# Eight of sixteen stretches of attention probabilities turned in blocks, the blocks carried by ScalarE and GpSimd

## The chip, the cores and the metric

The kernel runs on one NeuronCore of a Trainium2 chip. The core has a matrix engine (TensorE, PE in the profile), three engines for elementwise work (VectorE or DVE, ScalarE or ACT, GpSimd or POOL) and a queue engine that starts transfers (SyncE or SP). The metric is the device time of one execution in microseconds (us), as the median of three runs.

## The reference, cut to what matters

Two sequences of 512 tokens (here "trunks") go through one encoder layer with the same weights: a neighbourhood attention with 16 heads of 64 on a grid of 8 rows by 64 columns, then a mixture of 16 experts in which each expert picks its 64 best tokens of each trunk.

```
def trunk(x, ...):
    u = rmsnorm(h, norm_mix_g[i])
    mix = neighbourhood_attention(u, na_w_qkv[ia], na_rpb[ia], na_w_o[ia])
    h = h + mix
    u = rmsnorm(h, norm_ffn_g[i])
    h = h + expert_choice_ffn(u, router_w[i], moe_w_gate[i], moe_w_up[i], moe_w_down[i])
    return rmsnorm(h, final_norm_g)

def neighbourhood_attention(h, w_qkv, rpb, w_o):
    qkv = jnp.einsum('btd,de->bte', h, w_qkv)
    ...
        s = jnp.einsum('bchd,bicjhd->bhcij', q_r, k_win).astype(jnp.float32) + bias[None]
        p = jax.nn.softmax(s.reshape(B, NA_HEADS, GRID_W, kh * NA_KW), axis=-1)
        ...
        return jnp.einsum('bhcij,bicjhd->bchd', p, v_win)
    ...
    return jnp.einsum('btd,de->bte', out, w_o)
```

## The kernel before

**The parts.** The first 450 us or so are the attention of trunk 0 and then of trunk 1. The rest is the experts: sixteen passes over the weights, a loop of the same instructions. The change touches the attention alone.

**Precision.** Every float32 operand of a large product is split in two parts of a shorter format, a high part and a rest. ScalarE makes the high part (a cast, L870 for weights), VectorE the rest (a subtraction, L1404 for weights, `rest_pair`), and TensorE sums three products of parts. The weights come in slots of 128 x 2048 (a "pair": `q`, `k`, `v` or `w` with the number of its group); a slot is loaded again when its rest is made.

**Groups.** The 16 heads of a trunk go in four groups of four (`first_group` to `last_group`, one function on each engine). In each group TensorE projects the next group's queries and keys, and in turns the values (`project_v`) and the output (`project_out`). Within a group there are two pairs of heads (p = 0 and 1), and a pair is worked in two halves (hh = 0, 1 and hh = 2, 3). So there are 2 trunks x 4 groups x 2 pairs = 16 stretches.

**One stretch.** TensorE makes scores (`score`, L2193). VectorE adds the bias and takes the maximum (`biased`, L1478, L1482). ScalarE takes exponentials (`exponentials`, L895). VectorE multiplies with one over the sum (`normalise_rows`, L1498, L1501). Now the probabilities have queries on partitions, and the product with the values needs keys there: they have to be turned. There are two ways.
- In whole: TensorE transposes 28 pieces into PSUM (`turn_probabilities`, L2199), and VectorE and ScalarE copy one half each back to SBUF (`copy_pt`, L1486 and L900). 12 stretches go this way.
- In blocks: VectorE transposes blocks of 32 x 32 within their own 32 partitions (`turn_blocks_pt`, L1492), and ScalarE then carries 16 pieces of 32 partitions to the partitions where they belong (`move_pt`, L909). 4 stretches go this way, the first pair of the first and of the third group (`by_blocks`).

Then TensorE multiplies with the values (`values`, L2258), and the result is split (`split_ot`: high part by ScalarE, L934, rest by VectorE, L1518) for the output projection.

**Order.** Each engine runs its list in the order in which it is written, and waits on semaphores: `pt_dve`, `pt_act` and `pt_moved` say that turned probabilities are there, `norm_done` that normalised ones are. In the third group of trunk 0, ScalarE and VectorE also work out the root mean square of trunk 1's input (`next_piece`, `root`, `mean_square`, `one_over_rms`), for which ScalarE loads another table of functions (ACT_TABLE_LOAD). GpSimd does little in the attention: it clears a few tiles, starts transfers of its own queue, and waits.

Of the kernel before, what the change touches and what calls it, by code (L numbers as in the profile page):

```python
# [32 lines left out]
HEADS = 16  # L33
# [85 lines left out]
def by_blocks(n):  # L119

    return n % HEADS // GROUP % 2 == 0 and n % GROUP < PAIRED
# [59 lines left out]
ROW_BANKS = (4, 6)  # L181


def encoder_kernel(nc, x, x_t, g_mix, g_ffn_col, g_ffn, g_fin, w_qkv, bias, w_o, router_w, w_gate, w_up, w_down, identity, y):
# [5 lines left out]
    with ExitStack() as ctx:  # L190
# [3 lines left out]
        def sem(name):  # L194
            return ctx.enter_context(nc.semaphore(name))
# [231 lines left out]
        third_early, third_used = sem("third_early"), sem("third_used")  # L427
# [73 lines left out]
        def head_count(b, g):  # L501
            return HEADS * b + GROUP * g

# [210 lines left out]
        def _(pool):  # L714
# [11 lines left out]

            nc.gpsimd.memset(v[:, 0, 0:P], 0.0).then_inc(zeros_done, 1)
# [6 lines left out]
            pool.wait_ge(eps_done, 1 + QUARTERS)  # L734
            pool.wait_ge(piece_done, PIECES)
            nc.gpsimd.memset(ones_of[1], 1.0).then_inc(zeros_done, 1)
            for b in range(TRUNKS):

                if b:
                    pool.wait_ge(u_out, 16 * TILES * b)  # L740
                    pool.wait_ge(h_out, 16 * TILES * b)
                    pool.dma_start(*rows_of(xh, x, b)).then_inc(xh_in, 16)
                if b + 1 < TRUNKS:
# [122 lines left out]
        def _(act):  # L866
# [35 lines left out]
            def move_pt(A):  # L902

                act.wait_ge(pt_dve, A + PAIRED)
                for n in range(MOVES):
                    a, c = n % QUARTERS, n // QUARTERS
                    queries, keys = slice(a * QUARTER, (a + 1) * QUARTER), slice(c * QUARTER, (c + 1) * QUARTER)
                    into, of = arena[keys, 0:TILES:TILES - 1, a * WIN:(a + 1) * WIN], arena[queries, 1:TILES - 1, c * WIN:(c + 1) * WIN]
                    nc.scalar.copy(into, of).then_inc(pt_moved, 1)  # L909
# [136 lines left out]
            def second_group(b):  # L1046
                A = head_count(b, 1)
                exponentials(A, 0)
                exponentials(A, 1)
                cast_qk(b, 1, "q", 1)  # L1050
                cast_qk(b, 1, "k", 1)
                next_high(b, 1, None, "v", 2)
                copy_pt(A, 0)
                copy_pt(A, 1)
                if b == 0:
                    next_piece(2)
                    next_piece(3)
                next_high(b, 1, "w7", "v", 3)
                split_ot(A, 1, 0)
                exponentials(A, 2)  # L1060
                exponentials(A, 3)
                if b == 0:
                    next_piece(4)
                copy_pt(A, 2)
                copy_pt(A, 3)
                cast_qk(b, 2, "q", 0)
                cast_qk(b, 2, "k", 0)
                if b == 0:
                    next_piece(5)
                split_ot(A, 1, 1)  # L1070
                next_high(b, 1, "q1", "w", 1)

            def third_group(b):
# [16 lines left out]
                exponentials(A, 3)  # L1090
                if b == 0:
                    next_piece(8)
                    root(1)
                copy_pt(A, 2)
                copy_pt(A, 3)
                cast_qk(b, 3, "q", 0)
                cast_qk(b, 3, "k", 0)
# [139 lines left out]
            def highs(e, lo, hi):  # L1237

                for i in range(lo, hi):
# [3 lines left out]
                    if not split_first:  # L1243
                        act.wait_ge(pair_used, SLOTS * (q - FRONT_Q - 1) + i % SLOTS + 1)
                    elif i % SLOTS in THIRD_SLOTS:
                        act.wait_ge(third_used, 1)
# [24 lines left out]
            act.wait_ge(third_early, 1)  # L1271
            nc.scalar.activation(third_silu[0:CAP, :], bank(THIRD_BANKS[0])[CAP:P, :], ACT.Silu).then_inc(third_silu_done, 1)
            rows_high(0)
            act.wait_ge(third_used, 1)
# [125 lines left out]
        def _(dve):  # L1400
# [87 lines left out]
            def turn_blocks_pt(A, hh):  # L1488

                dve.wait_ge(norm_done, TILES * (A + hh + 1))  # L1490
                probabilities = scores[hh].rearrange("p i (c b j) -> p b (i c) j", c=2, b=QUARTERS)
                nc.vector.transpose(pt[hh], probabilities).then_inc(pt_dve, 1)  # L1492
# [136 lines left out]
            def second_group(b):  # L1629
# [16 lines left out]
                split_ot(b, g, 0)  # L1646
                biased(A, b, g, 2)
                biased(A, b, g, 3)
                rest_pair(b, "v", 2)
                normalise_rows(A, 2)  # L1650
                normalise_rows(A, 3)
                copy_q(b, g, 0)
                rest_pair(b, "v", 3)
                copy_k(b, g, 0)
                copy_pt(A, 2)
                copy_pt(A, 3)
                rest_qk(b, g + 1, "q", 0)
                rest_qk(b, g + 1, "k", 0)
                copy_q(b, g, 1)
                split_ot(b, g, 1)  # L1660

            def third_group(b):
# [291 lines left out]
            dve.wait_ge(third_used, 1)  # L1954
# [132 lines left out]
        def _(pe):  # L2087
# [195 lines left out]
            def second_group(b):  # L2283
# [13 lines left out]
                turn_probabilities(A, 2)  # L2297
# [7 lines left out]
            def third_group(b):  # L2305
# [13 lines left out]
                turn_probabilities(A, 2)  # L2319
# [312 lines left out]
            early_third(KC - 1, KC).then_inc(third_early, 1)  # L2632
# [5 lines left out]
            last.then_inc(third_used, 1)  # L2638
# [113 lines left out]
```

## Time and profile before

| | us |
|---|---|
| median of 3 runs (1519.72 to 1521.24) | 1520.5 |
| the profiled execution | 1520.91 |
| its span, first to last instruction | 1519.1 |
| TensorE busy in the span | 1505.3 |
| VectorE busy | 1316.2 |
| ScalarE busy | 1250.3 |
| GpSimd busy | 330.1 |

The mean granted TensorE clock was 0.999 of full speed. Busy time is a share over stages of different kinds: the two attentions (30 to 248 us and 248 to 448 us) have TensorE busy for 217.4 of 218.0 and 199.3 of 200.0 us, VectorE for 157.7 and 142.7, ScalarE for 138.8 and 105.0, GpSimd for 6.2 and 8.8. Matmuls are pipelined: one of 512 columns is shown with 0.39 us, but the next one starts 0.23 us after it. So the distance between starts is to be read, not the length. In the rows, times are us from the span's start, then the length in us, and "x" counts merged instructions.

### The profile page before, as it was taken

Reading aid. Unit: us, or ns where it says so; the run is one execution under the profiler, and the core shown is the slowest. Engines: PE = TensorE matmul, PEld = TensorE weight load, DVE = VectorE, ACT = ScalarE, POOL = GpSimd, SP = SyncE. Lnnn points to the kernel's source line nnn. Section 1 sums busy time; section 2 is a strip of 40 time slices with the busy share of each in tenths; the row PEclk is TensorE's granted clock in tenths of the full one; section 3 lists DMA queues with packets and bytes.
Section 4 is the critical chain, followed back from the end, with each engine's and each line's share of the span. In section 5 each row is a group of like instructions: output and inputs, shape, how many; then the busy total and the mean of one; then the engine's idle time right before and its main releaser. Section 6 shows DMA issues by size and latency. Waiting matters only on the chain.

```text
span 1519.1 us, 22067 instructions
## 1 busy us (share of the span) xinstructions
PE 1505.3 (99%) x7738; PEld 1217.5 (80%) x7738; DVE 1316.2 (87%) x1415; ACT 1250.3 (82%) x1491; POOL 330.1 (22%) x154
## 2 busy tenths in 40 slices
PE   9999999999999999999999999999999999999997
PEld 7888878888863888888888888888888888888886
DVE  7684786785865899999999999999999999999988
ACT  6756656546453799999999999999999999999997
POOL 0000001000022232242322523233242322420103
PEclk9999999999999999999999999999999999999999
DMA  9633447433476999999999999999999999999998
GB/s 346 193 137 124 154 140 265 124 125 111 151 248 225 395 420 391 415 400 404 407 406 405 397 411 391 398 407 399 412 388 404 405 393 414 395 414 382 387 396 349
DMA packets 156407, 498.59 MB, mean 328 GB/s; under 512 B 10880, under 2 KB 36608, under 8 KB 156352
## 3 DMA queue, kind: packets, MB, share of 16 engines
q1 hardware_dynamic: 144624, 461.54, 77.6%
q0 software_dynamic: 9280, 31.07, 6.6%
q10 hardware_dynamic: 2448, 5.25, 1.3%
q8 instruction: 34, 0.56, 0.1%
q14 instruction: 21, 0.17, 0.0%
HBM read 473.70 MB, written 20.97 MB: 326 GB/s over the span
## 4 chain that ended last, share of the span: by engine, by line
PE 89%; ACT 3%; DVE 3%; DMA 2%; issue 2%; SPq 0%; POOLq 0%; POOL 0%; ACTq 0%; DVEq 0%
PE ps L2093 76%; PE ps L2142 4%; PE ps L2149 2%; ACT w_high L1253 2%; PE ps L2258 2%; DVE w_rest L1404 2%; PE ps L2193 1%; PE ps L2414 1%; DMA raw<-w_gate 1%; PE ps L2199 1%; DMA u_rows<-arena 1%; ACT arena L1224 1%; DMA raw<-w_qkv 1%; PE ps L2696 0%; PE ps L2410 0%
## 5 line engine op out<-in xcount | busy, mean ns | idle before, releaser
L1404 DVE TENSOR_TENSOR w_rest<-raw,w_high 128x2048 fp32r<-128x2048 f32 x212 | 477.9, 2283 | 40.9 <-ACT w_high L1253 25.1
L1253 ACT CAST w_high<-raw 128x2048 fp32r<-128x2048 f32 x184 | 352.1, 1915 | 17.6 <-PE ps L2093 14.7
L2093 PE MATMUL ps<-w_high,xt_high 128*128 128x512 f32 x984 | 305.2, 390 | 0.7 <-DVE w_rest L1404 0.6
L2093 PE MATMUL ps<-w_rest,xt_high 128*128 128x512 f32 x984 | 304.3, 389 | 0.0
L2093 PE MATMUL ps<-w_high,xt_rest 128*128 128x512 f32 x984 | 304.2, 389 | 0.0
L2093 PEld LDWEIGHTS ps<-w_high,xt_high 128*128 128x128 f32 x984 | 184.1, 188 | 41.5 <-DVE w_rest L1404 2.4
L1404 DVE TENSOR_TENSOR w_rest<-early,w_high 128x2048 fp32r<-128x2048 f32 x90 | 204.4, 2286 | 13.3 <-ACT w_high L1253 13.3
L2093 PEld LDWEIGHTS ps<-w_high,xt_rest 128*128 128x128 f32 x984 | 184.7, 188 | 38.4
L2093 PEld LDWEIGHTS ps<-w_rest,xt_high 128*128 128x128 f32 x984 | 184.7, 188 | 38.3
L1404 DVE TENSOR_TENSOR w_rest<-raw_more,w_high 128x2048 fp32r<-128x2048 f32 x92 | 206.0, 2274 | 4.7 <-ACT w_high L1253 4.7
L1224 ACT COPY arena<-arena 32x256 f32<-32x256 f32 x464 | 187.3, 404 | 10.6
L1253 ACT CAST w_high<-early 128x2048 fp32r<-128x2048 f32 x90 | 172.2, 1915 | 10.9 <-PE ps L2093 8.9
L1253 ACT CAST w_high<-raw_more 128x2048 fp32r<-128x2048 f32 x92 | 175.8, 1912 | 2.9 <-PE ps L2093 1.9
L827 POOL DMA_INDIRECT h_rows<-xh,rows x15 | 109.5, 7302 | 303.4 <-ACT xh L1235 303.4
L784 POOL DMA_INDIRECT xh<-u_rows,aff x60 | 136.5, 2275 | 82.3 <-DVE v L1910 54.6
L2093 PE MATMUL ps<-ut_high,w_high 128*128 128x512 f32 x240 | 96.2, 401 | 0.3 <-DVE w_rest L1553 0.3
L2093 PE MATMUL ps<-ut_rest,w_high 128*128 128x512 f32 x240 | 93.7, 390 | 0.0
L2093 PE MATMUL ps<-ut_high,w_rest 128*128 128x512 f32 x240 | 93.6, 390 | 0.0
L895 ACT ACTIVATE arena<-arena,nmx 128x256 f32<-128x256 f32 x128 | 63.3, 496 | 33.4 <-DVE nmx L1482 33.4
L2093 PE MATMUL ps<-w_high,ht_high 128*128 128x512 f32 x256 | 78.9, 389 | 0.0
L2093 PE MATMUL ps<-w_high,ht_rest 128*128 128x512 f32 x256 | 78.8, 389 | 0.0
L2093 PE MATMUL ps<-w_rest,ht_high 128*128 128x512 f32 x256 | 78.8, 389 | 0.0
(319 smaller groups left out, 2304.0 us busy)
## 6 DMA issues: line engine op xcount, KB each, us to landing
raw<-w_down SPq DMA_DIRECT2D x64, 1024.0 KB, 8.8
raw<-w_gate SPq DMA_DIRECT2D x62, 1024.0 KB, 8.2
raw<-w_up SPq DMA_DIRECT2D x62, 1024.0 KB, 9.6
raw_more<-w_down SPq DMA_DIRECT2D x32, 1024.0 KB
early<-w_down SPq DMA_DIRECT2D x32, 1024.0 KB, 8.0
raw_more<-w_gate SPq DMA_DIRECT2D x31, 1024.0 KB
raw_more<-w_up SPq DMA_DIRECT2D x31, 1024.0 KB
early<-w_gate SPq DMA_DIRECT2D x31, 1024.0 KB, 9.5
```

The lines of the kernel that those rows point to most:

```text
L784: pool.indirect_dma_start(xg[:, t * SPAN:(t + 1) * SPAN], None, u_pieces, at).then_inc(gathered, 16)
L827: pool.indirect_dma_start(h_dram, bass.IndirectOffsetOnAxis(ap=rows[:, e:e + 1], axis=0), ys, None, compute_op=ALU.add).then_inc(scattered ...
L895: nc.scalar.activation(scores[hh % 2][:, i, :], scores[hh % 2][:, i, :], ACT.Exp, bias=nmx[:, hh % 2, i:i + 1], accum_out=psum_row[:, hh % ...
L1224: nc.scalar.copy(to_chunks[columns, :, tokens], from_blocks[tokens, :, columns]).then_inc(turn_step[h], 1)
L1253: nc.scalar.copy(w_high[:, i % SLOTS, :], src).then_inc(high_done, 1)
L1404: nc.vector.tensor_tensor(w_rest[:, j, :], src, w_high[:, j, :].bitcast(F32), ALU.subtract).then_inc(rest_done, 1)
L2093: done = nc.tensor.matmul(out, lhs, rhs, start=start and part == 0, stop=stop and part == 2)
L2142: nc.tensor.matmul(out[i], tokens[:, at], w_high[:, j:j + SHARED, kc * GC:(kc + 1) * GC], start=kc == 0 and tokens is ut_high, stop=False)
L2149: last = nc.tensor.matmul(out[i], ut_high[:, at], w_rest[:, j:j + SHARED, kc * GC:(kc + 1) * GC], start=False, stop=kc == KC - 1)
L2193: last = nc.tensor.matmul(bank(PAIR_BANKS[half], 2)[:, at + begin:at + end], queries[on, tile * P:(tile + 1) * P], keys[on, lo + begin:lo ...
L2199: return nc.tensor.transpose(bank(PAIR_BANKS[half] + r)[:, at:at + HD], scores[half][on, i, c * P:(c + 1) * P], ident[on, on])
L2258: last = nc.tensor.matmul(out, vals, probabilities[:, each * lo:each * hi, n, :], start=c == first, stop=c != first)
```

## The change

It has four parts.
- Two more stretches of each trunk are turned in blocks: the second pair of the second group and the second pair of the third group. `BY_BLOCKS` lists the four of a trunk, so eight of sixteen in all. The four calls of `turn_probabilities` there are gone, with the copies out of PSUM.
- In all eight, the 16 moves are shared: ScalarE carries pieces 0 to 7, GpSimd pieces 8 to 15, each GpSimd move waiting for the one before it. The value products wait for both (`pt_moved` and `pt_carried`).
- In those two groups VectorE does the second pair's bias ahead of the first pair's `split_ot`. The rests of the weights v2, v3 (second group) and w2, w3 (third group) move: v2 and w2 from in front of the normalisation to behind the transpositions, v3 and w3 to the group's end.
- In trunk 0's third group ScalarE does the last piece, the root and then a load of the exponentials' table behind the moves and the casts, and VectorE its mean square behind the rests of the next keys.

Two semaphores of the experts' start are merged into one; that moves nothing and is left out of the diff.

```diff
-    return n % HEADS // GROUP % 2 == 0 and n % GROUP < PAIRED
+    return (n % HEADS // GROUP, n % GROUP // PAIRED) in BY_BLOCKS
...
+BY_BLOCKS = ((0, 0), (1, 1), (2, 0), (2, 1))
...
+            def move_pt(A):
+
+                pool.wait_ge(pt_dve, A + PAIRED)
+                before = MOVES // 2 * turned_by_blocks(A) // PAIRED
+                for n in range(MOVES // 2):
+                    if n:
+                        pool.wait_ge(pt_carried, before + n)
+                    nc.gpsimd.tensor_copy(*block_of(MOVES // 2 + n)).then_inc(pt_carried, 1)
+                pool.wait_ge(pt_carried, before + MOVES // 2)
+
+            def move_blocks(b):
+                for g, p in BY_BLOCKS:
+                    move_pt(head_count(b, g) + PAIRED * p)
...
             pool.wait_ge(eps_done, 1 + QUARTERS)
+            move_blocks(0)
             pool.wait_ge(piece_done, PIECES)
...
                     pool.dma_start(*rows_of(xh, x, b)).then_inc(xh_in, 16)
+                    move_blocks(b)
...
-                for n in range(MOVES):
-                    a, c = n % QUARTERS, n // QUARTERS
-                    queries, keys = slice(a * QUARTER, (a + 1) * QUARTER), slice(c * QUARTER, (c + 1) * QUARTER)
-                    into, of = arena[keys, 0:TILES:TILES - 1, a * WIN:(a + 1) * WIN], arena[queries, 1:TILES - 1, c * WIN:(c + 1) * WIN]
-                    nc.scalar.copy(into, of).then_inc(pt_moved, 1)
+                for n in range(MOVES // 2):
+                    nc.scalar.copy(*block_of(n)).then_inc(pt_moved, 1)
...
                 exponentials(A, 3)
                 if b == 0:
                     next_piece(4)
-                copy_pt(A, 2)
-                copy_pt(A, 3)
+                move_pt(A + PAIRED)
                 cast_qk(b, 2, "q", 0)
                 cast_qk(b, 2, "k", 0)
...
                 exponentials(A, 3)
+                move_pt(A + PAIRED)
+                cast_qk(b, 3, "q", 0)
+                cast_qk(b, 3, "k", 0)
                 if b == 0:
                     next_piece(8)
                     root(1)
-                copy_pt(A, 2)
-                copy_pt(A, 3)
-                cast_qk(b, 3, "q", 0)
-                cast_qk(b, 3, "k", 0)
+                    nc.scalar.preload_act_table(ACT.Exp)
                 split_ot(A, 2, 1)
...
-                split_ot(b, g, 0)
                 biased(A, b, g, 2)
                 biased(A, b, g, 3)
+                split_ot(b, g, 0)
+                normalise_rows(A, 2)
+                turn_blocks_pt(A, 2)
+                normalise_rows(A, 3)
+                turn_blocks_pt(A, 3)
+                copy_q(b, g, 0)
                 rest_pair(b, "v", 2)
-                normalise_rows(A, 2)
-                normalise_rows(A, 3)
-                copy_q(b, g, 0)
-                rest_pair(b, "v", 3)
                 copy_k(b, g, 0)
-                copy_pt(A, 2)
-                copy_pt(A, 3)
                 rest_qk(b, g + 1, "q", 0)
                 rest_qk(b, g + 1, "k", 0)
                 copy_q(b, g, 1)
+                rest_pair(b, "v", 3)
                 split_ot(b, g, 1)
...
-                split_ot(b, g, 0)
                 biased(A, b, g, 2)
                 biased(A, b, g, 3)
+                split_ot(b, g, 0)
+                normalise_rows(A, 2)
+                turn_blocks_pt(A, 2)
+                normalise_rows(A, 3)
+                turn_blocks_pt(A, 3)
+                copy_q(b, g, 0)
+                copy_k(b, g, 0)
                 rest_pair(b, "w", 2)
-                normalise_rows(A, 2)
-                normalise_rows(A, 3)
+                rest_qk(b, g + 1, "q", 0)
+                rest_qk(b, g + 1, "k", 0)
                 if b == 0:
                     mean_square(1)
-                copy_q(b, g, 0)
+                split_ot(b, g, 1)
                 rest_pair(b, "w", 3)
-                copy_k(b, g, 0)
-                copy_pt(A, 2)
-                copy_pt(A, 3)
-                rest_qk(b, g + 1, "q", 0)
-                rest_qk(b, g + 1, "k", 0)
-                split_ot(b, g, 1)
                 if b == 0:
                     one_over_rms(1, True)
...
-                    pe.wait_ge(pt_moved, MOVES * (turned_by_blocks(A) // PAIRED + 1))
+                    carried = MOVES // 2 * (turned_by_blocks(A + hh - half) // PAIRED + 1)
+                    pe.wait_ge(pt_moved, carried)
+                    pe.wait_ge(pt_carried, carried)
...
                 project_t(b, g, "q0", q)
                 project_t(b, g, "k0", k)
-                turn_probabilities(A, 2)
                 project_t(b, g, "q1", q)
...
                 project_t(b, g, "k0", k)
-                turn_probabilities(A, 2)
                 project_t(b, g, "q1", q, 0, KC // 2)
```

In the rows of the order, a row is an engine's instruction with its line, its output and inputs and its shape, and "x" counts equal ones in a row.

VectorE in trunk 0's third group, from the second half's normalisation to the reciprocal root, before (L1404 is a weight's rest, L1486 a copy out of PSUM, L1518 `split_ot`):

```order
L1501 TENSOR_SCALAR arena<-arena,rinv 128x256 x4
L1435 TENSOR_REDUCE ssq<-ssq 128x4
L1443 TENSOR_SCALAR var<-ssq 128x4
L1511 SCALAR_TENSOR_TENSOR early<-ps,grow 128x512
L1404 TENSOR_TENSOR w_rest<-raw,w_high 128x2048
L1506 TENSOR_TENSOR early<-ps,grow 128x512
L1486 COPY arena<-ps 128x512 x2
L1572 TENSOR_TENSOR qk<-early,qk 128x512 x2
L1518 TENSOR_TENSOR ot_rest<-ps,ot_high 128x512
L1454 RECIPROCAL newt<-sdev 128x4
```

and now (L1512 is the transposition in blocks, L1424 a weight's rest, L1538 `split_ot`):

```order
L1518 RECIPROCAL rinv<-psum_row 128x4
L1521 TENSOR_SCALAR arena<-arena,rinv 128x256 x4
L1512 STREAM_TRANSPOSE arena<-arena 128x1024
L1531 SCALAR_TENSOR_TENSOR early<-ps,grow 128x512
L1526 TENSOR_TENSOR early<-ps,grow 128x512
L1424 TENSOR_TENSOR w_rest<-raw,w_high 128x2048
L1592 TENSOR_TENSOR qk<-early,qk 128x512 x2
L1455 TENSOR_REDUCE ssq<-ssq 128x4
L1463 TENSOR_SCALAR var<-ssq 128x4
L1538 TENSOR_TENSOR ot_rest<-ps,ot_high 128x512
L1424 TENSOR_TENSOR w_rest<-raw,w_high 128x2048
L1474 RECIPROCAL newt<-sdev 128x4
```

The first weight's rest (w2, which stood ahead of both normalisations) is now between the copies of q and k and the rests of the next queries and keys, the second (w3) between `split_ot` and the reciprocal root, behind which the next group's bias begins; the mean square follows the rests of queries and keys.

ScalarE in the same group, from the second pair's exponentials to the next group's, before:

```order
L895 ACTIVATE arena,psum_row<-arena,nmx 128x256 x8
L954 ACTIVATE piece,ssq<-piece 128x512
L890 ACT_TABLE_LOAD
L890 ACTIVATE sdev<-var 128x4
L900 COPY arena<-ps 128x512 x2
L916 CAST qk<-early 128x512 x2
L934 CAST ot_high<-ps 128x512
L895 ACT_TABLE_LOAD
L895 ACTIVATE arena,psum_row<-arena,nmx 128x256 x8
```

and now (L930 are the moves, L937 casts of the next queries and keys, L955 the high part of `split_ot`):

```order
L919 ACTIVATE arena,psum_row<-arena,nmx 128x256 x8
L930 COPY arena<-arena 32x2x256 x8
L937 CAST qk<-early 128x512 x2
L975 ACTIVATE piece,ssq<-piece 128x512
L914 ACT_TABLE_LOAD
L914 ACTIVATE sdev<-var 128x4
L1117 ACT_TABLE_LOAD
L955 CAST ot_high<-ps 128x512
L919 ACTIVATE arena,psum_row<-arena,nmx 128x256 x8
```

The last piece, the table load and the root stood ahead of the copies; they now stand between the casts and `split_ot`, and the second table load moved from behind `split_ot` to ahead of it.

## Rows read from the trace of the kernel before

**Rows 1.** Page, parts 1 and 4: busy us (share) and count by engine; the chain by engine.

```profile
PE 1505.3 (99%) x7738; PEld 1217.5 (80%) x7738; DVE 1316.2 (87%) x1415; ACT 1250.3 (82%) x1491; POOL 330.1 (22%) x154
...
PE 89%; ACT 3%; DVE 3%; DMA 2%; issue 2%; SPq 0%; POOLq 0%; POOL 0%; ACTq 0%; DVEq 0%
```

**Rows 2.** Waits of TensorE, 0 to 500 us: total us, times, longest; the first of seven.

```profile
PE ps L2468 <- ACT ut_high L1132: 1.2, 1, 1.2
```

**Rows 3.** TensorE in time order, trunk 0's third group: start us, length us.

```profile
160.84 1.60 PE L2193 MATMUL ps<-qk 64*128 64x184 f32 x24
162.37 0.50 PE L2093 MATMUL ps<-ut_high,w_high 128*128 128x512 f32 x1
...
173.18 0.39 PE L2093 MATMUL ps<-ut_high,w_rest 128*128 128x512 f32 x1
173.49 1.08 PE L2199 MATMUL ps<-ident,arena 64*128 64x64 f32 x28
...
174.84 0.39 PE L2093 MATMUL ps<-ut_rest,w_high 128*128 128x512 f32 x1
...
177.45 0.55 PE L2258 MATMUL ps<-arena,v 128*64 128x128 f32 x8
...
189.08 1.08 PE L2199 MATMUL ps<-ident,arena 64*128 64x64 f32 x28
```

**Rows 4.** VectorE in the same stretch.

```profile
162.29 0.42 DVE L1478 CUSTOM_DVE_ANT_0 arena<-ps,bias_more 128x256 f32<-128x256 f32 x1
...
165.51 2.28 DVE L1404 TENSOR_TENSOR w_rest<-raw,w_high 128x2048 fp32r<-128x2048 f32 x1
...
169.06 0.16 DVE L1498 RECIPROCAL rinv<-psum_row 128x4 f32<-128x4 f32 x1
169.25 1.14 DVE L1501 TENSOR_SCALAR arena<-arena,rinv 128x256 f32<-128x256 f32 x4
...
179.88 0.69 DVE L1518 TENSOR_TENSOR ot_rest<-ps,ot_high 128x512 fp32r<-128x512 f32 x1 [2.72 <-ACT ot_high L934]
...
181.50 0.42 DVE L1478 CUSTOM_DVE_ANT_0 arena<-ps,bias_sb 128x256 f32<-128x256 f32 x1
...
187.50 1.14 DVE L1501 TENSOR_SCALAR arena<-arena,rinv 128x256 f32<-128x256 f32 x4
```

**Rows 5.** ScalarE in the same stretch.

```profile
163.99 0.51 ACT L895 ACTIVATE arena<-arena,nmx 128x256 f32<-128x256 f32 x1 [2.35 <-DVE nmx L1482]
...
167.94 0.62 ACT L954 ACTIVATE piece<-piece 128x512 f32<-128x512 f32 x1
168.67 1.28 ACT L890 ACT_TABLE_LOAD   x1
170.70 0.20 ACT L890 ACTIVATE sdev<-var 128x4 f32<-128x4 f32 x1 [0.74 <-DVE var L1443]
...
179.26 0.59 ACT L934 CAST ot_high<-ps 128x512 fp32r<-128x512 f32 x1 [2.90 <-PE ps L2258]
```

**Rows 6.** VectorE and ScalarE, trunk 0's first group: transposing and moving blocks.

```profile
42.30 2.37 DVE L1492 STREAM_TRANSPOSE arena<-arena 128x1024 f32<-128x1024 f32 x2
...
44.70 10.26 ACT L909 COPY arena<-arena 32x512 f32<-32x512 f32 x16 [0.75 <-DVE arena L1492]
```

**Rows 7.** GpSimd's groups by shape (busy us, mean ns), and the copies in time.

```profile
L837 POOL CAST xt_high<-v 128x1024 fp32r<-128x1024 f32 x14 | 14.6, 1045 | 128.2 <-DVE w_rest L1404 128.2
...
L792 POOL COPY v<-ident 32x128 f32<-32x128 f32 x4 | 1.2, 292 | 0.2
...
455.77 1.35 POOL L792 COPY v<-ident 32x128 f32<-32x128 f32 x4
```

**Rows 8.** GpSimd beside VectorE at the kernel's end, in time order.

```profile
1499.45 1.22 DVE L2032 CUSTOM_DVE_ANT_0 xh<-arena 128x1024 f32<-128x1024 f32 x1
...
1499.97 2.96 POOL L858 TENSOR_TENSOR arena<-arena,grow 128x1024 f32<-128x1024 f32 x1 [17.83 <-ACT xh L873]
1502.91 7.04 POOL L858 TENSOR_TENSOR h_more<-h_more,grow 128x1024 f32<-128x1024 f32 x3
```

More of the change, by code:

```diff
@@ L426, in encoder_kernel @@
         third_in = [sem(f"third_in{m}") for m in range(2)]
-        third_early, third_used = sem("third_early"), sem("third_used")
+        third_mm = sem("third_mm")
+        pt_carried = sem("pt_carried")
         third_silu_done, third_hid_done = sem("third_silu_done"), sem("third_hid_done")
@@ L502, in head_count, with block_of @@
             return HEADS * b + GROUP * g
+        def block_of(n):
+            a, c = n % QUARTERS, n // QUARTERS
+            queries, keys = slice(a * QUARTER, (a + 1) * QUARTER), slice(c * QUARTER, (c + 1) * QUARTER)
+            return (arena[keys, 0:TILES:TILES - 1, a * WIN:(a + 1) * WIN], arena[queries, 1:TILES - 1, c * WIN:(c + 1) * WIN])
         @block.sync
@@ L1245, in highs @@
                     elif i % SLOTS in THIRD_SLOTS:
-                        act.wait_ge(third_used, 1)
+                        act.wait_ge(third_mm, 2)
                     if split_first:
@@ L1270, in _ @@
             nc.scalar.copy(by_trunk(xt_high)[:, 0, :, :], by_chunk[0]).then_inc(xth_done, 1)
-            act.wait_ge(third_early, 1)
+            act.wait_ge(third_mm, 1)
             nc.scalar.activation(third_silu[0:CAP, :], bank(THIRD_BANKS[0])[CAP:P, :], ACT.Silu).then_inc(third_silu_done, 1)
             rows_high(0)
-            act.wait_ge(third_used, 1)
+            act.wait_ge(third_mm, 2)
             nc.scalar.activation(third_silu[CAP:P, :], bank(THIRD_BANKS[0])[0:CAP, :], ACT.Silu).then_inc(third_silu_done, 1)
@@ L1490, in turn_blocks_pt @@
                 dve.wait_ge(norm_done, TILES * (A + hh + 1))
-                probabilities = scores[hh].rearrange("p i (c b j) -> p b (i c) j", c=2, b=QUARTERS)
-                nc.vector.transpose(pt[hh], probabilities).then_inc(pt_dve, 1)
+                probabilities = scores[hh % 2].rearrange("p i (c b j) -> p b (i c) j", c=2, b=QUARTERS)
+                nc.vector.transpose(pt[hh % 2], probabilities).then_inc(pt_dve, 1)
             def normalise_rows(A, hh):
@@ L1953, in _ @@
             first_rest_of_rows(1)
-            dve.wait_ge(third_used, 1)
+            dve.wait_ge(third_mm, 2)
             dve.wait_ge(third_silu_done, 2)
@@ L2631, in _ @@
             first_rows()
-            early_third(KC - 1, KC).then_inc(third_early, 1)
+            early_third(KC - 1, KC).then_inc(third_mm, 1)
             pe.wait_ge(first_xt_done, 1)
@@ L2637, in _ @@
                 _, last = whole_gate_up(late_xt, kc, 2, slice(0, CAP), slice(CAP, P), kc == 0, kc == KC - 1)
-            last.then_inc(third_used, 1)
+            last.then_inc(third_mm, 1)
             places()
```

## Prediction

> **What bounds the kernel now.** I read the page first, then the stages, then TensorE's waits, then the three engines side by side in one stretch. The page says that TensorE is busy 99% of the span, and that the chain that ended last is TensorE for 89% [rows 1]. In the first 500 us, where the change lies, its longest wait for another engine is 1.2 us [rows 2], and that one comes before any attention. So a TensorE instruction that goes is worth its whole time, and whatever another engine delivers later than TensorE asks for it costs its whole lateness. The question is therefore how much slack stands behind the four turns that are removed. TensorE's rows of trunk 0's third group show the stretch [rows 3]: scores of the second pair (L2193), 48 projection products for q0 and k0, the 28 transposes (L2199), 12 products for half of q1, the value products (L2258), then 36 products until the next turn at 189.08. A projection product starts every 0.23 us.
>
> **What goes.** Four turns go (second pair of the second and third group, in both trunks). One costs the time from the last product ahead of it (173.18) to the second product behind it (174.84), less two steps of 0.23: 1.66 - 0.45 = 1.21 us [rows 3]. Four make 4.84 us. On ScalarE and VectorE eight half copies each out of PSUM go too, but neither of them is waited for, so that is worth nothing by itself. The value products read another layout in the same number of instructions; TensorE's time for them is put at no change. That leaves -4.84 us if nothing comes late.
>
> **What is asked earlier or later.** I follow trunk 0's third group on the clock of the trace of before.
>
> VectorE's bias starts when the first score half is there, at about 161.9 (12 of the 24 score products in [rows 3], and the last one's own 0.25 us), and no longer behind ot_rest at 162.29 [rows 4]. The two bias sets hold VectorE 3.2 us (162.29 to 165.51), so until 165.1; ot_rest takes 0.6, until 165.7. ScalarE's exponentials end 5.65 us after the first bias row (162.29 to 167.94 [rows 4, 5]), so at 167.55, the first half of them two microseconds earlier. Then VectorE normalises (0.2 + 1.06 us from [rows 4]) and transposes (2.37 us for two [rows 6]): 165.7 + 1.26 + 1.15 + 1.26 + 1.22 gives 170.65 for the second transposition. Both carriers start there.
>
> ScalarE moves sixteen blocks in 10.26 us [rows 6], so eight in 5.13, until 175.8. TensorE asks for the values at 177.45 - 1.21 = 176.24. That half is in time by 0.4 us.
>
> GpSimd has no such move in the trace. The nearest rows: 292 ns for a copy of 128 elements on 32 partitions, 1045 ns for 1024 elements on 128 partitions, and 1.35 us for four copies that wait for each other as these do [rows 7]. That is 0.84 ns an element and 0.34 us a step at 128 elements, so 0.34 + 384 x 0.84 ns = 0.66 us a move, an estimate. Eight take 5.3 us, until 176.0: in time by 0.2 us, with nothing to spare. Bounds: 0.43 a move (512 x 0.84 ns) if the fixed part overlaps with the move before it, 0.9 if moving between partition groups costs as much again as a short copy's fixed part (0.24 us, from the same two rows); below 0.62 it makes no difference, since ScalarE's half and the projection then decide.
>
> **Where GpSimd meets VectorE.** At the kernel's end GpSimd starts a product at 1499.97, half a microsecond into a VectorE instruction that reads two operands from SBUF (1499.45, 1.22 us), and takes 2.96 us; the three products behind it, beside VectorE instructions with one SBUF operand, take 7.04 / 3 = 2.35 [rows 8]. The extra 0.6 us is what VectorE had left. So I take it that a GpSimd instruction is held until such a VectorE instruction ends. I take the hold to work both ways, since what the two share would be the same; if only GpSimd is held, half a microsecond goes off each wait below. The Trainium skill (SBUF — State Buffer, "Who interferes with whom") calls it an exclusive lock and adds the other direction, that VectorE is held behind a GpSimd instruction that started first. Of the page's two directions the trace agrees with the one; no row here shows the other. With the one alone the sum would be about 1 us lower.
>
> What VectorE does while the moves run is then decisive. In the third group it copies q0 and then k0, whose last product starts at 173.18 [rows 3], until 174.2. Then comes w2's rest, 2.2 us with two SBUF operands. Five moves and part of the sixth are done by then; the sixth ends at 174.65, the rest runs until 176.9, and two moves remain. They meet the rests of q0 and k0 (0.65 us each). Alternating, the last move ends at 179.0; behind both rests, at 179.6. I take 179.0: TensorE waits 2.8 us (at most 3.4) for the values, in each trunk.
>
> In the second group TensorE does 12 products more ahead of the values, 2.7 us, and VectorE's chain is 0.3 us later after its start, because ScalarE first finishes a cast. Moves start 10.1 us after the scores' start, values are asked for at 18.1. Without a meeting the moves end at 15.4: no wait. With v2's rest (2.2) right behind q0's copy, and later the rests of q0 and k0 (0.65 each), they end at 19.0: 0.9 us late in trunk 0, and 0.5 in trunk 1, where ScalarE is free 0.35 us earlier. Together 1.4 us.
>
> In the first pair of the first and third group the moves are shared as well. There TensorE has two whole value projections (and in the third group the output's) to do before it asks, so I cost that at nothing; if GpSimd met every rest of w there, it would add under 10 us to a wait that has more than that in hand.
>
> **The moved rest of w3.** It leaves the stretch ahead of the turn and now stands between ot_rest (179.88) and the next group's first bias (181.50 [rows 4]). On that chain TensorE's next turn depends: normalisation of the second half ends at 187.50 + 1.14 = 188.64 [rows 4], and TensorE asks for it 12 transposes into the turn of 189.08, at 189.5 [rows 3]. Slack 0.9 us; 2.2 us come in. Alone that is 1.3 us in trunk 0. Trunk 1 has no reciprocal root on that chain (1.0 us between ot_rest's end and the bias), so 0.3 us there.
>
> In trunk 0 the square root comes on top. ScalarE now does it behind the moves: two casts (0.6 each, by the nearest cast of this shape, 179.26), the last piece (0.73 from 167.94 to 168.67), a table load of 1.28, the root of 0.2 and a second table load [rows 5], and only then ot_high, which before started 1.81 us after the values' start (177.45 to 179.26). Without any meeting: 175.8 + 1.1 + 0.73 + 1.28 + 0.2 + 1.28 = 180.4, where ot_high would be wanted at 178.05. From there ot_high 0.62, ot_rest 0.62, w3's rest 2.2, the reciprocal root 1.0, and 7.14 from bias to normalised: 192.0. TensorE asks at 176.24 + 12.06 = 188.3. It waits 3.7 us. With the meeting, VectorE's mean square ends at 180.0, ScalarE is free at 181.5, normalised at 193.1; TensorE, itself late, asks at 191.1 and waits 2.0. Either way trunk 0's third group loses 3.7 to 4.8 us.
>
> The other moved steps cost nothing by themselves. v3's rest is needed only by the next value projection, half of whose products run first; it delays the next bias by 0.6 us, in front of a pair with much slack. The SP loads into the slots of v2, v3, w2 and w3 start 3 to 10 us later, each for weights that only a later group or the experts use. GpSimd's own queue holds a memset and loads behind the moves; none is wanted before the last group.
>
> **The sum.** -4.84 + 1.4 (second groups) + 4.8 (trunk 0's third group) + 2.8 + 0.3 (trunk 1's) = +4.5 us. The profiled run took 1520.9 us, 0.4 over the median, so 1525.4 on its own time and **1525.0 on the median**.
>
> **Rivals.**
> 1. *GpSimd and VectorE don't hold each other when GpSimd only copies.* For it: the one row that shows the hold is a product with two operands. Against it: a copy reads SBUF too. Then only the w3 and root terms remain: -4.84 + 3.7 + 0.3 = -0.8, **1519.7**, not slower. It decides at the values: no wait there.
> 2. *The hold exists, but GpSimd keeps its string and VectorE waits.* GpSimd's next move follows 0.05 us after the last one. Then w2's rest starts at 176.0, the rests of q0 and k0 end at 179.5, and the next scores, wanted at 177.9, wait 1.6 us in each trunk; the root's chain costs 3.1. Net +1.5, **1522.0**.
> 3. *Nothing comes late.* If w3's rest and the root find room that I don't see, the removed turns remain: 1515.7 at best, **1516.5** with a few tenths lost. Against it: the slack of 0.9 us in [rows 3, 4].
> 4. *GpSimd's move is dearer*, 0.9 us: moves end 1.5 to 2 us later in all four stretches, and the sum comes to about **1530**.
> That the change does not do what it says I leave out: the order of instructions shows eight moves on each carrier.
>
> **How the numbers follow.** Forecast 45%, rival 1 25%, rival 2 12%, rival 3 10%, rival 4 8%. The range of 1518.5 to 1529 leaves out rival 3 and the dear end of rival 4. A change under 0.2%, 3 us, can't be told from none: faster is below 1517.5 (rival 3), the same is 1517.5 to 1523.5 (rivals 1 and 2), slower the rest (forecast and rival 4).
>
> **What would show it.** The profile of the changed kernel should have 224 transposes at the line of the turns instead of 336. TensorE should wait at the value products of the second pairs for GpSimd's moves (about 0.5 to 1 us in the second, 3 us in the third groups), and at the last groups' first turn for VectorE's normalisation (2 us in trunk 0). GpSimd's moves should be about 0.6 us each, those beside a rest of w about 2 us longer or later. Ot_high of trunk 0's third group should start right behind a table load. I am wrong if the moves run at an even spacing through VectorE's rests, if TensorE shows no wait at the turn behind w3's rest, or if a move takes far from 0.66 us.

## The result, and the profile after

The changed kernel takes 1525.25 us (median of 7 runs, 1524.18 to 1525.89), the kernel before 1520.41 beside it: 1.0031 times as long, 95% interval 1.0019 to 1.0043. That is the forecast's side and, within 0.3 us, its number. The profiled run took 1524.21 us (span 1522.4), at the fast end of its runs: its trace holds 3.3 us of the 4.8 between the medians.

Parts 1 and 4 of the page of the changed kernel, to be held against [rows 1]:

```profile
PE 1501.7 (99%) x7626; PEld 1215.0 (80%) x7626; DVE 1327.5 (87%) x1415; ACT 1249.1 (82%) x1483; POOL 392.8 (26%) x218
...
PE 86%; DVE 5%; ACT 4%; DMA 2%; issue 2%; SPq 0%; POOLq 0%; POOL 0%; ACTq 0%; DVEq 0%
```

TensorE has lost 112 instructions and 3.6 us of work, and yet the span grew: the chain that ended last now runs through VectorE and ScalarE more often. Where, the waits of TensorE in the first 500 us say (the answer to [rows 2]; total us, times, longest):

```profile
PE ps L2280 <- issue: 5.9, 3, 2.8
PE ps L2219 <- DVE arena L1521: 1.2, 1, 1.2
PE ps L2213 <- DVE qk L1592: 0.7, 3, 0.3
```

L2280 are the value products, which wait for the two semaphores of the carriers; L2219 are the turns, L2213 the scores. Trunk 0's third group on TensorE, as [rows 3], from the values on:

```profile
177.57 0.55 PE L2280 MATMUL ps<-arena,v 128*64 128x128 f32 x8 [2.82 <-issue]
...
189.19 0.58 PE L2219 MATMUL ps<-ident,arena 64*128 64x64 f32 x12
191.01 0.71 PE L2219 MATMUL ps<-ident,arena 64*128 64x64 f32 x16 [1.24 <-DVE arena L1521]
```

The row marked "issue" has no releaser of its own, so the carriers have to be read beside it. GpSimd there: the eight moves, one of the first five alone, and the sixth alone.

```profile
169.42 8.05 POOL L742 COPY arena<-arena 32x512 f32<-32x512 f32 x8 [31.17 <-DVE arena L1512]
...
170.77 0.61 POOL L742 COPY arena<-arena 32x512 f32<-32x512 f32 x1
...
172.79 2.65 POOL L742 COPY arena<-arena 32x512 f32<-32x512 f32 x1
```

VectorE in the same stretch, as [rows 4]: the copy of k0, w2's rest, the rests of q0 and k0, the mean square, ot_rest, w3's rest, the first bias of the next group.

```profile
172.07 0.69 DVE L1526 TENSOR_TENSOR early<-ps,grow 128x512 f32<-128x512 f32 x1 [2.20 <-PE ps L2113]
172.68 2.28 DVE L1424 TENSOR_TENSOR w_rest<-raw,w_high 128x2048 fp32r<-128x2048 f32 x1
175.14 1.85 DVE L1592 TENSOR_TENSOR qk<-early,qk 128x512 fp32r<-128x512 f32 x2 [0.18 <-ACT qk L937]
176.91 0.15 DVE L1455 TENSOR_REDUCE ssq<-ssq 128x4 f32<-128x8 f32 x1
...
179.99 0.69 DVE L1538 TENSOR_TENSOR ot_rest<-ps,ot_high 128x512 fp32r<-128x512 f32 x1 [2.49 <-ACT ot_high L955]
180.59 2.28 DVE L1424 TENSOR_TENSOR w_rest<-raw,w_high 128x2048 fp32r<-128x2048 f32 x1
...
183.81 0.42 DVE L1498 CUSTOM_DVE_ANT_0 arena<-ps,bias_sb 128x256 f32<-128x256 f32 x1
```

ScalarE, as [rows 5]: its eight moves, the table load, the root, the second table load, ot_high.

```profile
169.32 5.14 ACT L930 COPY arena<-arena 32x512 f32<-32x512 f32 x8 [3.24 <-DVE arena L1512]
...
176.27 1.28 ACT L914 ACT_TABLE_LOAD   x1
177.56 0.21 ACT L914 ACTIVATE sdev<-var 128x4 f32<-128x4 f32 x1
177.79 1.28 ACT L1117 ACT_TABLE_LOAD   x1
179.37 0.59 ACT L955 CAST ot_high<-ps 128x512 fp32r<-128x512 f32 x1 [0.30 <-PE ps L2280]
```

ScalarE's half is done at 174.46, GpSimd's at 177.47, and TensorE, ready at 174.75, starts 0.10 behind GpSimd's. The sixth move was issued at 172.79, a tenth behind the start of w2's rest, and ends half a microsecond behind that rest's end: 2.65 us where the others take 0.61. In return the rests of q0 and k0 take 1.85 us beside the last two moves, where they take 1.28 alone (in the run with w2's rest in quarters, below). The copy of k0, which has only one operand in SBUF, holds nothing up: the fifth move, beside it, takes 0.61 us. Trunk 1 shows the same numbers (values at 400.19 after 2.82 us).

### The profile page after: what moved, and what is told of

Same layout as the page of the kernel before. It is cut to its first block, busy times and chain, and to the rows that moved or that the text cites. A ratio compares the mean times of both kernels' runs of the same rounds, so it can differ in the third digit from the quotient of the medians.

```text
span 1522.4 us, 21912 instructions
## 1 busy us (share of the span) xinstructions
PE 1501.7 (99%) x7626; PEld 1215.0 (80%) x7626; DVE 1327.5 (87%) x1415; ACT 1249.1 (82%) x1483; POOL 392.8 (26%) x218
## 4 chain that ended last, share of the span: by engine, by line
PE 86%; DVE 5%; ACT 4%; DMA 2%; issue 2%; SPq 0%; POOLq 0%; POOL 0%; ACTq 0%; DVEq 0%
PE ps L2113 74%; PE ps L2162 4%; DVE w_rest L1424 2%; PE ps L2169 2%; ACT w_high L1273 2%; PE ps L2280 2%; PE ps L2213 1%; PE ps L2434 1%; DMA raw<-w_gate 1%; DMA u_rows<-arena 1%; DVE arena L1498 1%; ACT arena L919 1%; ACT arena L1244 0%; DMA raw<-w_qkv 0%; PE ps L2716 0%
## 5 line engine op out<-in xcount | busy, mean ns | idle before, releaser
L1424 DVE TENSOR_TENSOR w_rest<-raw,w_high 128x2048 fp32r<-128x2048 f32 x212 | 479.4, 2290 | 38.1 <-ACT w_high L1273 25.3
L1424 DVE TENSOR_TENSOR w_rest<-early,w_high 128x2048 fp32r<-128x2048 f32 x90 | 204.4, 2286 | 13.2 <-ACT w_high L1273 13.1
L1424 DVE TENSOR_TENSOR w_rest<-raw_more,w_high 128x2048 fp32r<-128x2048 f32 x92 | 206.0, 2274 | 4.7 <-ACT w_high L1273 4.7
L742 POOL COPY arena<-arena 32x512 f32<-32x512 f32 x64 | 61.9, 967 | 260.9 <-DVE arena L1512 257.5
L842 POOL TENSOR_TENSOR xh<-xh,grow 128x1024 f32<-128x1024 f32 x15 | 36.2, 2410 | 194.3 <-DVE w_rest L1424 192.2
```

The costliest lines, as they stand in the source:

```text
L742: nc.gpsimd.tensor_copy(*block_of(MOVES // 2 + n)).then_inc(pt_carried, 1)
L842: nc.gpsimd.tensor_tensor(tokens, tokens, weights, ALU.mult).then_inc(rows_scaled, 1)
L1424: nc.vector.tensor_tensor(w_rest[:, j, :], src, w_high[:, j, :].bitcast(F32), ALU.subtract).then_inc(rest_done, 1)
```

## The experiments

Seven runs were made: six altered kernels, and the changed kernel once more. The edits are to the changed kernel unless it is said otherwise; differences are to its 1525.25 us and to its trace, and "times before" is the ratio to the kernel before.

### w3's rest into VectorE's gap

```diff
-                split_ot(b, g, 1)
                 rest_pair(b, "w", 3)
+                split_ot(b, g, 1)
```

> Theory (w3's rest in front of the next group's bias is what makes the turn late, in trunk 0 and in trunk 1): with w3's rest ahead of ot_rest, where VectorE stands idle 2.5 us in trunk 0 and 3.0 us in trunk 1, the first bias of the last group starts about 2.2 us sooner, TensorE's wait at that group's first turn (1.24 us in trunk 0, 0.33 us in trunk 1) is gone, the waits at the values of the third groups stay at 2.8 us: about 1.6 us off the changed kernel, 1523.7. Rival (the root's chain and the late values set that turn, the rest of w3 lies beside them): the wait at the turn stays at 1.2 us and the time at 1525.2.

1524.07 us (10 runs, 1522.42 to 1525.28; 1.0025 times the kernel before, 1.0015 to 1.0034). The wait at the turn is gone in both trunks: no row of L2219 waits. But the median fell by 1.2 us, not 1.6, and the profiled run (1523.79) by 0.4. Its TensorE rows show why:

```profile
177.46 0.91 PE L2280 MATMUL ps<-arena,v 128*64 128x128 f32 x8 [2.82 <-issue]
...
190.56 1.08 PE L2219 MATMUL ps<-ident,arena 64*128 64x64 f32 x28
```

The eight products that took 0.55 us take 0.91. By stretch (length, TensorE busy, granted clock, DMA share, GB/s), first the changed kernel, then this one:

```profile
177.00:180.00 3.00, 2.43 (x44) 1.00 0.81 287
```

```profile
177.00:180.00 3.00, 2.54 (x26) 0.51 0.81 287
180.00:183.00 3.00, 3.00 (x38) 0.92 0.79 222
```

The granted clock fell to its lower level, 1.2 GHz, at the end of the same wait of 2.82 us that had left it at 2.4 GHz in the changed kernel's profile, and stayed there until about 180.5; in trunk 1 again. This term is in no part of the prediction.

It also blurs what this run says about w3's rest. VectorE's ot_rest and the first bias of the next group in this run:

```profile
181.32 0.69 DVE L1538 TENSOR_TENSOR ot_rest<-ps,ot_high 128x512 fp32r<-128x512 f32 x1 [1.75 <-ACT ot_high L955]
...
182.94 0.42 DVE L1498 CUSTOM_DVE_ANT_0 arena<-ps,bias_sb 128x256 f32<-128x256 f32 x1
```

From the start of ot_rest to the bias it is 1.62 us, where the changed kernel has 3.82 (179.99 to 183.81): the 2.2 us of w3's rest are off the chain to the turn. But ot_rest itself came 1.3 us later, so the bias came 0.9 us sooner and not 2.2, and TensorE, slowed by the clock, reached the turn 1.4 us later (190.56 for 189.19), which by itself covers the 1.24 us. So the rest's place on the chain is shown; that it alone made the turn late is not shown by this wait's end in trunk 0. The run with all three moved, at the full clock, has no wait there either.

### w2's rest ahead of the second pair's bias

```diff
                 add_out(b, g, "w", 4, 8)
+                rest_pair(b, "w", 2)
                 biased(A, b, g, 2)
...
                 copy_k(b, g, 0)
-                rest_pair(b, "w", 2)
```

> Only w2's rest moves, ahead of the second pair's bias, where VectorE waits 1.9 us for the scores; no rest of w then meets the moves of the third group. Theory (hold): GpSimd's eight moves run at an even spacing of 0.68 us and end about 5.4 us after their start (now 8.05), the values wait at most 0.4 us instead of 2.82 in both trunks. Trunk 1 gains all of it, about 2.4 us. Trunk 0 gains only about 0.7, since there the table loads and the root, which lay beside the late values, now end last, and the wait at the next turn grows from 1.24 to about 3 us. Sum about 1522. Rival A (no hold, the moves are slow by themselves or the late side is another): values still wait 2.8 us, 1525.2 or more. Rival B (hold, but nothing comes behind it): both trunks gain 2.4, 1520.4.

1522.45 us (11 runs; 1.0015 times before, 1.0006 to 1.0024): 2.8 off, 3.2 expected. GpSimd, TensorE's values and turns, and ScalarE in trunk 0:

```profile
169.54 5.32 POOL L742 COPY arena<-arena 32x512 f32<-32x512 f32 x8 [31.33 <-DVE arena L1512]
```

```profile
174.95 0.55 PE L2280 MATMUL ps<-arena,v 128*64 128x128 f32 x8 [0.30 <-issue]
...
188.94 0.89 PE L2219 MATMUL ps<-ident,arena 64*128 64x64 f32 x12 [2.27 <-DVE arena L1521]
190.80 1.12 PE L2219 MATMUL ps<-ident,arena 64*128 64x64 f32 x16 [0.97 <-DVE arena L1521]
...
206.83 1.08 PE L2219 MATMUL ps<-ident,arena 64*128 64x64 f32 x28
```

```profile
177.66 0.20 ACT L914 ACTIVATE sdev<-var 128x4 f32<-128x4 f32 x1
177.89 1.28 ACT L1117 ACT_TABLE_LOAD   x1
179.18 0.59 ACT L955 CAST ot_high<-ps 128x512 fp32r<-128x512 f32 x1
```

Without the meeting the eight moves take 5.32 us and not 8.05, and the values wait 0.30: one instruction of VectorE cost 2.5 us in each trunk. This decides against rival 1 of the prediction (no hold). In trunk 0 ot_high now stands right behind the second table load, as the prediction said, and the turn waits 2.27 + 0.97 = 3.24 us in place of 1.24: most of what came off the values is lost at the turn. The rest goes too, and more, since behind these waits the granted clock fell (length, TensorE busy, granted clock, DMA share, GB/s):

```profile
189.00:192.00 3.00, 2.03 (x29) 0.50 0.43 172
```

It stayed low until about 195.8, and the turn behind that starts at 206.83, where the changed kernel has:

```profile
206.15 1.08 PE L2219 MATMUL ps<-ident,arena 64*128 64x64 f32 x28
```

So in this profile trunk 0 came out 0.7 us later and didn't gain the 0.7 that was expected. Trunk 1, which has no root there, keeps its 2.5 us. And the kernel is still slower than the one before: without the meeting at w2's rest the waits at trunk 0's turn, 3.24 us, alone take back more than its two removed turns had brought (2.42).

### w2's rest in quarters

```diff
-                rest_pair(b, "w", 2)
...
+                for part in range(4):
+                    at = slice(part * PAIR // 4, (part + 1) * PAIR // 4)
+                    piece_of = nc.vector.tensor_tensor(w_rest[:, j, at], raw[:, j, at], w_high[:, j, at].bitcast(F32), ALU.subtract)
+                piece_of.then_inc(rest_done, 1)
```

> w2's rest stays in its place but is issued as four instructions of 512 columns (about 0.6 us each) in place of one of 2048 (2.28 us). Theory (GpSimd is held for the length of one VectorE instruction and gets its turn between two): the sixth, seventh and eighth move each wait about 0.6 us for a quarter, not 2 us for the whole; the eight moves end about 6 us after their start (8.05 in the changed kernel), the rest of w is drawn out instead, and TensorE waits 0.6 to 0.9 us at the values of the third groups instead of 2.82. Trunk 1 gains 2 us, trunk 0 little (the table loads and the root end last there, as in the run with w2's rest early): about 1523. Rival A (VectorE keeps the way as long as its instructions follow each other): one move still takes 2.6 us, the values wait 2.8. Rival B (GpSimd keeps it through its string of moves): moves end 5.4 us after the start, w2's rest begins only then, and the rests of q0 and k0, and with them the next scores, are late.

1523.29 us (10 runs; 1.0019 times before, 1.0010 to 1.0029). GpSimd, then VectorE, then TensorE's values in both trunks:

```profile
169.30 6.49 POOL L742 COPY arena<-arena 32x512 f32<-32x512 f32 x8 [31.08 <-DVE arena L1512]
...
173.81 0.95 POOL L742 COPY arena<-arena 32x512 f32<-32x512 f32 x1
```

```profile
172.59 3.73 DVE L1716 TENSOR_TENSOR w_rest<-raw,w_high 128x512 fp32r<-128x512 f32 x4
176.25 1.28 DVE L1592 TENSOR_TENSOR qk<-early,qk 128x512 fp32r<-128x512 f32 x2
```

```profile
175.89 0.55 PE L2286 MATMUL ps<-arena,v 128*64 128x128 f32 x8 [1.22 <-issue]
...
399.99 0.55 PE L2286 MATMUL ps<-arena,v 128*64 128x128 f32 x8 [1.22 <-issue]
```

The two engines take turns: a move gets in between two quarters and takes about 1 us with its wait, the four quarters together 3.73 us instead of 2.28. The wait at the values falls from 2.82 to 1.22 us (0.6 to 0.9 expected; the moves wait a little longer than half a quarter). So the hold lasts for one instruction, and neither side keeps it over its string: rivals A and B fall, and with B the prediction's rival 2. In trunk 0 the turn then waits twice, as with w2's rest early:

```profile
189.12 0.59 PE L2225 MATMUL ps<-ident,arena 64*128 64x64 f32 x12 [1.56 <-DVE arena L1521]
190.98 1.12 PE L2225 MATMUL ps<-ident,arena 64*128 64x64 f32 x16 [1.28 <-DVE arena L1521]
```

Behind the first of these waits the clock fell, until about 197; behind the 1.22 us at the values it stayed at the upper level.

### All three moved

w2's rest as above and w3's as in the first run; on ScalarE the root and its two table loads go behind ot_high, on VectorE the reciprocal root to the last group.

```diff
                     next_piece(8)
-                    root(1)
-                    nc.scalar.preload_act_table(ACT.Exp)
                 split_ot(A, 2, 1)
+                if b == 0:
+                    root(1)
+                    nc.scalar.preload_act_table(ACT.Exp)
...
+                    one_over_rms(1, True)
                     diagonals(b + 1)
```

> w2's rest as in the run before; w3's rest ahead of ot_rest; trunk 1's square root and its two table loads behind ot_high on ScalarE, which is idle 5.5 us there; the reciprocal root ahead of the diagonals of the last group. Theory: the waits at the values of the third groups (2.82 us each) fall to 0.4 or less and the waits at the turns behind them (1.24 and 0.33 us) go: about 6.4 us off the changed kernel, 1518.8, which is 1.6 under the kernel before. Rival (VectorE is full from the bias of the last group on, so that what is taken from the turn comes back at its copies and sums, where TensorE waits 0.35 us now): half of the gain in trunk 0 is lost again, 1521.

1517.74 us (11 runs, 1517.35 to 1518.47; 0.9984 times before, 0.9975 to 0.9993): faster than both kernels, and 1.1 under what was expected. The values wait 0.28 and 0.30 us, no turn waits. The granted clock stays at its upper level through the attention. One new wait stands later in trunk 0, of the kind the rival named:

```profile
209.81 0.50 PE L2113 MATMUL ps<-w_high,ut_high 128*128 128x512 f32 x1 [1.40 <-DVE xh L1545]
```

That the missing falls of the clock are the 1.1 us is likely, not shown. The spread of the runs doesn't settle it: it is 1.1 us here and 1.7 to 2.9 in the four kernels before this one, but also 2.7 in the run with only the second groups, whose profile has no fall in the attention.

### The reciprocal root between two normalisations

The edit is to the kernel with all three moved.

```diff
                 normalise_rows(A, 0)
+                if b == 0:
+                    one_over_rms(1, True)
                 normalise_rows(A, 1)
...
-                    one_over_rms(1, True)
                     diagonals(b + 1)
```

> As the run with all moved, but the reciprocal root stands between the normalisations of the last group's first pair, where VectorE is idle 0.6 us, and no longer behind the copies of the next pair, where TensorE waited 1.40 us for a sum of VectorE. Theory: that wait was the reciprocal root's 1.0 us in front of the sum, so it goes to 0.4 or less, and the normalisation of the second half is at most 0.4 us later, which TensorE's turn does not see or sees with 0.2 us: 1.0 to 1.4 us off 1517.7, 1516.5. Rival (the sum is late because of the rest of the next trunk's weights ahead of it, not because of the root): the wait stays at 1.4 us, 1517.7.

1517.03 us (11 runs; 0.9979 times before, 0.9970 to 0.9988). The wait fell from 1.40 to 0.33 us, so it was the reciprocal root's. Scores wait 0.28 us more, and TensorE waits for a load (a transfer) behind the attention 0.8 us instead of 0.4, so 0.7 us of the 1.1 arrive. This is the best version measured.

### Only the second groups

The second pair of the third groups is turned by TensorE again, in the order of the kernel before.

```diff
-BY_BLOCKS = ((0, 0), (1, 1), (2, 0), (2, 1))
+BY_BLOCKS = ((0, 0), (1, 1), (2, 0))
```

> The second groups as in the changed kernel, the second pair of the third groups turned by TensorE again, in the order of the kernel before. Two turns of 1.21 us are gone, 2.4 us. By the prediction's price for the second groups (1.4 us of waits) the time is 1519.4; by what the changed kernel's trace shows there (0.27 us in trunk 0, none in trunk 1) it is 1518.2. Rival (the gain of the second groups is given back in the third groups, because v3's rest and the first pair's shared moves come later): 1520.4 or more, with a wait at the values or scores of the third groups' first pair.

1519.61 us (11 runs, 1517.69 to 1520.41; 0.9994 times before, 0.9985 to 1.0003). The interval includes 1, and by the time alone this would speak for the dear price. The traces say otherwise. TensorE's last instructions, before and here:

```profile
1504.10 7.05 PE L2696 MATMUL ps<-early,xh 128*128 128x512 f32 x24
```

```profile
1501.16 7.05 PE L2717 MATMUL ps<-early,xh 128*128 128x512 f32 x24
```

TensorE is done 2.94 us sooner: the two turns (2.42) and half a microsecond of a load's wait (0.9 before, 0.4 here). The longest wait at the values is 0.2 us, and neither values nor scores of the third groups' first pair wait, so the rival falls. The end of the chain that ended last, GpSimd's last write of y, before and here:

```profile
1514.14 0.02 POOLq L861
1514.15 0.84 issue
1514.99 1.24 POOLq L190
```

```profile
1511.19 0.02 POOLq L885
1511.21 2.27 issue
1513.48 1.24 POOLq L191
```

There 1.43 us are given back, in GpSimd's issue of the last write; in the other eight profiles (of before, after and the six other runs) it takes 0.79 to 0.84. Why it was long here, and how often, one profile can't say; it stays open. The profiled run (1519.37) lies near the median of its runs, and only two of the eleven (1517.69 and 1518.32) come near the 1517.9 that it would have had without this.

### The changed kernel once more

> The changed kernel once more, nothing altered, for a second profile. Its runs lie at 1524.2 (two) and at 1525.0 to 1525.9 (five), and the one profiled lay at 1524.2 with the clock at its upper level throughout the third groups. In the run with w3's rest ahead of ot_rest the granted clock fell to half behind both 2.82 us waits, for about 3 us each. Theory (a wait of this length sometimes lets the clock fall, and that is the 1.2 us between the profile and the median): this profile, if its time is 1525 or more, shows the granted clock at 0.5 for about 3 us behind one of the two waits, at a price of 1.2 to 1.5 us; if its time is 1524.2 it shows none. Rival (the spread comes from the experts' stage): time 1525 or more with the clock at 1.0 behind both waits.

One run, 1527.2 us, 1.3 above the slowest of the first seven. Its stretch behind the wait in trunk 1, and the products in it:

```profile
402.00:405.00 3.00, 3.00 (x33) 0.51 0.60 239
```

```profile
401.82 0.91 PE L2280 MATMUL ps<-arena,v 128*64 128x128 f32 x8 [2.82 <-issue]
```

Behind trunk 0's wait the clock was low as well (mean 0.62 from 180 to 184). From the values to the next turn TensorE takes 13.25 us in trunk 1 (401.82 to 415.07) where the first profile has 11.74 (400.19 to 411.93): 1.5 us for one fall. In trunk 0 it is 1.6, but there the turn's own wait shrinks from 1.24 to 0.19, so 0.6 is left. With a wait of 0.7 us for a copy of v that the first profile lacks, this makes up 2.8 of the 3.0 us between the two profiles. So the clock accounts for 2.1 us between these two executions of one kernel. What it does to the other runs isn't shown: their mean clocks are on record with three digits, where a fall of 3.4 us is one in the last, and they don't sort the times (0.998 at 1524.21 and at 1525.49 us, 0.997 at 1524.18 and at 1525.32).

## Why the prediction was right, step by step

- **The four turns, -4.84.** Right. The run with the second groups alone shows two of them as 2.94 less 0.5 us.
- **GpSimd's move, 0.66 us.** Right: 0.61 us each, one every 0.675. Rival 4 falls.
- **The hold, both ways.** Right, and the largest loss. The third groups' values wait 2.82 us in both trunks; 2.8 was forecast. The order differs a little: the prediction had the sixth move ahead of w2's rest, in the trace the rest is 0.1 us ahead and the move is held. The hold at w2's rest doesn't decide the sign by itself, as rival 1 would have it (1519.7 without any hold): without that meeting the time was 1522.45, with the turn's 3.24 us and a fall of the clock in it. The Trainium skill (SBUF — State Buffer, "Who interferes with whom") states both directions, and the trace now agrees with both: 2.65 against 0.61 us for the move, 1.85 against 1.28 for the two rests.
- **The second groups, 1.4.** Wrong in size: 0.27 in trunk 0, none in trunk 1. GpSimd's eight moves beside v2's rest end 18.3 us after the scores' start (97.66 to 115.99); the prediction had 19.0, against the 18.1 at which the values are asked for. It charged a full 2.2 us for v2's rest and 0.65 for each of the two later rests; in the trace the eight moves take 7.96 us, 2.6 over the 5.32 of an unmet string, and the two rests bore part (1.78 us for 1.28).
- **w3's rest, 1.3 and 0.3.** Right in size: 1.24 in trunk 0, and in trunk 1 the 27 transposes of the turn take 1.41 us instead of 1.08.
- **The root on top, 2.0 at the turn together with w3's rest.** The chain exists (ot_high behind the table load in the run with w2's rest early, 3.24 us at the turn, 3.7 forecast for that case), but in the changed kernel the late values hide it: ot_high waits for TensorE, not for the table. The prediction had the mean square end at 180.0 on the clock of before, 178.6 on this one, and ran the root and the second table load after it; it ended at 177.5, beside the first load, because w2's rest, and with it all that follows on VectorE, came ahead of the sixth move. So trunk 0's third group lost 2.82 + 1.24, not 4.8.
- **The sum.** The profile has +3.3 us for a forecast of +4.5: 1.1 too much in the second groups and 0.8 at the turn, and on the other side 0.7 that it didn't count. These 0.7 are a net: four later waits that are longer by 0.3 to 0.4 us each, 1.3 together, less 0.4 at the load behind the attention and some 0.5 by which TensorE is ahead before the attention begins; the wait of 1.2 us of [rows 2] isn't in this profile, and no run shows that the change has a part in that. So in the profile, which has no fall of the clock, the forecast for the profiled run, 1525.4, is 1.2 us too high, and the second profile of the same kernel, with two falls, lies 1.8 above it. The mechanisms were right, but that the median meets the forecast within 0.3 us is luck: two terms were too high, others were left out, among them the fall of the clock behind the long waits. How much of the median is that fall isn't recorded.
- **A slip in the chain.** 165.7 + 1.26 + 1.15 + 1.26 + 1.22 is 170.59, not 170.65; nothing depends on the 0.06.

## What to carry to other kernels

Before work is given to GpSimd, look up which VectorE instructions with two SBUF operands run in that stretch: one such instruction of 2.3 us cost the whole 2.4 us that a trunk's two removed turns had brought, and moving it into a gap of VectorE gave them back in trunk 1. Then follow the next chain in line, since in trunk 0 the time saved at the values turned up at the next turn until the root and w3's rest were moved too. And where TensorE gets waits as long as those here (2.27 and 2.82 us at once, or 1.56 and 1.28 close together), count a possible fall of the clock as well as the wait.

## What the runs showed of the hardware

- VectorE and GpSimd take turns instruction by instruction: four quarters of 512 columns and three moves interleave, 3.73 us in place of 2.28 for the quarters, about 1 us for a move in place of 0.61. A copy of VectorE with one operand in PSUM (0.69 us) left the move beside it at 0.61.
- Around waits of TensorE of 2.82 us, busy before, the granted clock went to 0.5 for 3.4 us in two profiles (w3's rest into the gap, the changed kernel once more) and stayed at 1.0 in another of the changed kernel with the same waits: about 1.5 us for each fall. Where two waits stood close together at a turn (2.27 and 0.97, 1.56 and 1.28) it was low for 6.8 us.
